# Triangular inversions on 64-wide diagonal blocks with a halved solve, and levels up to block 16 on four 32-wide tiles

## What is computed

```python
A = jnp.where(strict, jnp.einsum('bnhid,bnhjd->bnhij', kb, k) * gamma, 0.0)
T = lax.linalg.triangular_solve(A + eye, jnp.broadcast_to(eye, A.shape), left_side=True, lower=True, unit_diagonal=True)
u = T @ (v * beta[..., None])
w = T @ (kb * jnp.exp(g)[..., None])
...
def step(S, inp):
    u_n, w_n, qk_n, qd_n, kd_n, gt_n = inp
    v_new = u_n - jnp.einsum('bhck,bhkv->bhcv', w_n, S)
    o = jnp.einsum('bhck,bhkv->bhcv', qd_n, S) + jnp.einsum('bhij,bhjv->bhiv', qk_n, v_new)
    S = S * gt_n[..., None, None] + jnp.einsum('bhck,bhcv->bhkv', kd_n, v_new)
    return S, o
```

## Time and profile before

| | us |
|---|---|
| median of 3 runs | 2135.83 |
| lowest and highest | 2133.89, 2140.08 |
| the profiled execution, its own time | 2136.59 |
| its span in the trace | 2134.8 |
| TensorE busy in it | 1933.7 |
| VectorE busy in it | 606.0 |
| ScalarE busy in it | 316.7 |

### The profile page before, as it was taken

One profiled execution on the slowest core, in us unless ns is written; L12 is line 12 of the kernel. 1 busy time (PEld: TensorE's weight loads), 2 busy tenths in 40 slices (PEclk: granted clock), 3 DMA queues, 4 the chain that ended last, 5 costly groups with the idle time before them and its releaser, 6 DMA issues. The chain is left out here.

```text
span 2134.8 us, 36739 instructions
## 1 busy us (share of the span) xinstructions
PE 1933.7 (91%) x16513; PEld 1559.3 (73%) x16513; DVE 606.0 (28%) x1266; ACT 316.7 (15%) x639; POOL 41.1 (2%) x65
## 2 busy tenths in 40 slices
PE   5898987978999989878888879999999999999996
PEld 3786877877788868768787744456996699669953
DVE  4436565553200024635655310000000000100002
ACT  1012122220000014322222110000001100110011
POOL 0001000000000000000000000000000000000000
PEclk9999998989999999988999879999999999999999
DMA  9719431010443324100000079799999999999994
GB/s 352 281 63 427 171 158 80 1 80 9 158 158 147 129 112 174 40 6 11 11 11 6 1 322 387 276 390 428 425 421 420 428 425 417 428 426 425 408 429 191
DMA packets 37119, 492.75 MB, mean 231 GB/s; under 512 B 4379, under 2 KB 4540, under 8 KB 7324
## 3 DMA queue, kind: packets, MB, share of 16 engines
q1 hardware_dynamic: 36956, 490.33, 55.8%
HBM read 487.95 MB, written 2.36 MB: 230 GB/s over the span
## 5 line engine op out<-in xcount | busy, mean ns | idle before, releaser
L1946 PE MATMUL bank<-ring,arena 128*32 128x128 f32 x2016 | 227.6, 273 | 0.0
L1943 PE MATMUL bank<-ring,arena 128*32 128x384 f32 x2016 | 224.8, 487 | 2.5 <-DMA ring<-in_experts 2.5
L1946 PEld LDWEIGHTS bank<-ring,arena 128*32 128x32 f32 x2016 | 217.9, 110 | 0.0
L1938 PE MATMUL bank<-ring,arena 128*64 128x256 f32 x1792 | 204.8, 381 | 2.4 <-DMA ring<-in_experts 2.4
L1938 PEld LDWEIGHTS bank<-ring,arena 128*64 128x64 f32 x1792 | 126.2, 137 | 79.8 <-issue 22.7
L2140 DVE TENSOR_TENSOR arena<-bank,arena 128x256 f32<-128x256 f32 (+2 forms) x56 | 28.4, 508 | 545.3 <-PE bank L1946 154.8
L1229 PE MATMUL bank<-arena,ring 128*128 128x256 f32 x704 | 155.3, 382 | 4.0 <-DVE arena L290 3.8
L1229 PEld LDWEIGHTS bank<-arena,ring 128*128 128x128 f32 x704 | 134.0, 191 | 24.5 <-issue 4.1
L2096 ACT ACTIVATE arena<-bank 128x256 f32<-128x256 f32 (+2 forms) x56 | 25.3, 451 | 699.3 <-PE bank L1946 294.4
L1350 PE MATMUL bank<-arena,ring 128*128 128x256 f32 x512 | 115.6, 388 | 6.4 <-DVE arena L290 3.8
L1350 PEld LDWEIGHTS bank<-arena,ring 128*128 128x128 f32 x512 | 98.6, 194 | 24.8 <-issue 5.8
(11 more groups left out here) (368 smaller groups left out, 2506.3 us busy)
## 6 DMA issues: line engine op xcount, KB each, us to landing
ring<-in_experts SPq DMA_DIRECT2D x168, 2048.0 KB, 20.3
ring<-in_stream SPq DMA_DIRECT2D x61, 2048.0 KB, 11.0
arena<-in_masks SPq DMA_DIRECT2D x1, 1280.0 KB, 5.3
xT<-in_xT SPq DMA_DIRECT2D x1, 1024.0 KB, 6.1
arena<-in_s0gd SPq DMA_DIRECT2D x4, 256.0 KB, 3.3
out_sgd<-arena SPq DMA_DIRECT2D x4, 256.0 KB, 2.5
out_y<-arena SPq DMA_DIRECT2D x4, 256.0 KB, 2.5
arena<-in_hfw SPq DMA_DIRECT2D x1, 544.0 KB
```

The costliest lines, as they stand in the source:

```text
L1938: mm = nc.tensor.matmul(out[HALF * x:HALF * x + HALF, 0:256], h[:, j, 0:HALF], w[:, j, 256 * x:256 * x + 256], start=start, stop=stop, til ...
L1943: nc.tensor.matmul(out[lo:hi, 0:3 * P], h[:, j, lo:hi], w[:, j, 0:3 * P], start=start, stop=stop, tile_position=(0, lo), skip_group_check= ...
L1946: mm = nc.tensor.matmul(out[MID:P, r * P:(r + 1) * P], h[:, j, 32 * r:32 * r + 32], w[:, j, 3 * P:4 * P], start=(start and r == 0), stop=s ...
```

## The change

The inversion is now made on the two diagonal blocks of 64 of each 128 by 128 matrix. T, U and X hold two blocks on top of each other: 128 partitions, 64 columns for each q. LEVELS falls from 7 to 6, so levels 1 to 5 remain, and level 5 has the short form that level 6 had. Masks, copies and the strict scores shrink to 64 columns for each q (256 columns for four q instead of 512).

`pe_level` splits each product along the diagonal. For l up to 4 (blocks up to 16 joined into 32) it issues four matmuls of 32 by 32 with 32 columns on the tiles (0,0), (32,32), (64,64), (96,96) of the array; for l = 5 two of 64 by 64 with 64 columns on (0,0) and (64,64).

The rest of the triangular system is done by `pe_solve` in three steps: the diagonal blocks multiply the right-hand side; the off-diagonal block of A multiplies the solved half (one tile, (64a, 64b)); the other diagonal block multiplies that and adds to the first result in PSUM. After each step the half that is needed is copied, for g = 0 by ACT (`act_solve`), for g = 1 by DVE (`dve_solve`). The width of the right-hand side is 64 columns in the RWKV stage and 128 in the DeltaNet stage.

In the RWKV stage the right-hand sides are formed after level 3, in bank 7; TensorE waits there for the key norm of the next round (`s_krt`), and ACT copies both after both are done. The strict scores (now L998) are two matmuls of 64 by 64 columns on two column tiles instead of one of 128 by 128.

```diff
         class Inversion:
-            def __init__(self):
-                self.T = [take(4, T) for _ in range(2)]
-                self.U = [take(4, T) for _ in range(2)]
-                self.X = [take(4, T) for _ in range(2)]
+
+            def __init__(self, n):
+                self.n = n
+                self.T = [take(4, HB64) for _ in range(2)]
+                self.U = [take(4, HB64) for _ in range(2)]
+                self.X = [take(4, HB64) for _ in range(2)]
+                self.H = [take(4, n)] * 2
+                self.Z = [take(4, n) for _ in range(2)]
                 self.final = [self.U[0], self.T[1]]
...
             def dve_first(self, dve, r, g, low, up):
 
                 dve.wait_ge(s_id[g], 2 * (r + 1))
-                nc.vector.copy_predicated(self.T[g], self.level_mask(0, 0), low).then_inc(s_T[g], 1)
-                nc.vector.copy_predicated(self.U[g], self.level_mask(1, 0), up).then_inc(s_U[g], 1)
+                for dst, src, upper, done in ((self.T[g], low, 0, s_T[g]), (self.U[g], up, 1, s_U[g])):
+                    for rows, part in src:
+                        ins = nc.vector.copy_predicated(dst[rows], self.level_mask(upper, 0, rows), part)
+                    ins.then_inc(done, 1)
 
             def pe_level(self, pe, r, l, up):
+                w = 32 if 2 << l <= 32 else HB64
+                parts = [(slice(o, o + w), slice(o % HB64, o % HB64 + w), (o, o)) for o in range(0, P, w)]
+                column = lambda q, c: slice(q * HB64 + c.start, q * HB64 + c.stop)
                 for g in range(2):
                     pe.wait_ge(s_T[g], r * NT[g] + l)
                     for q in range(4):
-                        mm = nc.tensor.matmul(ps[g][:, q * T:(q + 1) * T], up[g][:, q], self.T[g][:, q], start=True, stop=True)
+                        for rows, c, at in parts:
+                            mm = nc.tensor.matmul(ps[g][rows, column(q, c)], up(g, q, rows, c), self.T[g][rows, q, c],
+                                                  start=True, stop=True, tile_position=at)
                     mm.then_inc(s_X[g], 1)
                 for g in range(2):
                     pe.wait_ge(s_U[g], r * NU[g] + l)
                     pe.wait_ge(s_Xs[g], r * (LEVELS - 1) + l)
                     if l < LEVELS - 1 or g == 1:
                         for q in range(4):
-                            mm = nc.tensor.matmul(ps[2 + g][:, q * T:(q + 1) * T], self.U[g][:, q], self.X[g][:, q],
-                                                  start=True, stop=True)
+                            for rows, c, at in parts:
+                                mm = nc.tensor.matmul(ps[2 + g][rows, column(q, c)], self.U[g][rows, q, c], self.X[g][rows, q, c],
+                                                      start=True, stop=True, tile_position=at)
                         mm.then_inc(s_TX[g], 1)
                     if l < LEVELS - 1 or g == 0:
                         for q in range(4):
-                            mm = nc.tensor.matmul(ps[4 + g][:, q * T:(q + 1) * T], self.X[g][:, q], self.U[g][:, q],
-                                                  start=True, stop=True)
+                            for rows, c, at in parts:
+                                mm = nc.tensor.matmul(ps[4 + g][rows, column(q, c)], self.X[g][rows, q, c], self.U[g][rows, q, c],
+                                                      start=True, stop=True, tile_position=at)
                         mm.then_inc(s_XU[g], 1)
 
...
-            def pe_final(self, pe, r, g):
-                pe.wait_ge(s_U[0] if g == 0 else s_T[1], (r + 1) * LEVELS)
-
-
+                                                  ps[4 + g][:, 0:4 * HB64].rearrange("p (q t) -> p q t", q=4)).then_inc(s_U[g], 1)
+
+            def pe_solve(self, pe, r, rhs, rhs_ready, lower):
+
+                n = self.n
+                for g in range(2):
+                    pe.wait_ge(s_U[0] if g == 0 else s_T[1], (r + 1) * LEVELS)
+                    rhs_ready(g)
+                    for q in range(4):
+                        for h in range(2):
+                            mm = nc.tensor.matmul(ps[g][blk(h), q * n:(q + 1) * n], self.final[g][blk(h), q], rhs[g][blk(h), q],
+                                                  start=(q == 0), stop=False, tile_position=(HB64 * h, HB64 * h), skip_group_check=True)
+                    mm.then_inc(s_Z[g], 1)
+                for g in range(2):
+                    a, b = g, 1 - g
+                    pe.wait_ge(s_Zs[g], 3 * r + 1)
+                    for q in range(4):
+                        mm = nc.tensor.matmul(ps[2 + g][blk(b), q * n:(q + 1) * n], lower[g][blk(a), q, blk(b)], self.Z[g][blk(a), q],
+                                              start=True, stop=True, tile_position=(HB64 * a, HB64 * b))
+                    mm.then_inc(s_Z[g], 1)
+                for g in range(2):
+                    b = 1 - g
+                    pe.wait_ge(s_Zs[g], 3 * r + 2)
+                    for q in range(4):
+                        mm = nc.tensor.matmul(ps[g][blk(b), q * n:(q + 1) * n], self.final[g][blk(b), q], self.H[g][blk(b), q],
+                                              start=False, stop=True, tile_position=(HB64 * b, HB64 * b), skip_group_check=True)
+                    mm.then_inc(s_Z[g], 1)
+
+            def solution_part(self, eng, r, g, k):
+
+                rows = blk(g if k == 0 else 1 - g)
+                dst = (self.H if k == 1 else self.Z)[g][rows].rearrange("p q v -> p (q v)")
+                eng.wait_ge(s_Z[g], 3 * r + k + 1)
+                return dst, ps[2 + g if k == 1 else g][rows, 0:4 * self.n]
+
+            def act_solve(self, act, r):
+                for k in range(3):
+                    dst, src = self.solution_part(act, r, 0, k)
+                    nc.scalar.activation(dst, src, ACT.Copy).then_inc(s_Zs[0], 1)
+
+            def dve_solve(self, dve, r):
+                for k in range(3):
+                    dst, src = self.solution_part(dve, r, 1, k)
+                    nc.vector.tensor_copy(dst, src).then_inc(s_Zs[1], 1)
+
+            def solved(self, eng, r):
+                for g in range(2):
+                    eng.wait_ge(s_Zs[g], 3 * r)
 
         drop(m_rw)
         m_keep = floats[0]
-        inv = Inversion()
+        inv = Inversion(RWN)
...
+                        if l == RHS_LEVEL:
+                            act.wait_ge(s_G, 2 * c + 2)
+                            for g in range(2):
+                                nc.scalar.activation(Gs[g].rearrange("p q v -> p (q v)"), ps[7][:, g * TT:(g + 1) * TT], ACT.Copy)\
+                                    .then_inc(s_Gs, 1)
+                    inv.act_solve(act, c)
...
-                            mm = nc.tensor.matmul(ps[4 + hh][:, s * T:(s + 1) * T], ar[g][:, 0, tok], bk[hh][:, 0, tok],
-                                                  start=True, stop=True)
+                            for h in range(2):
+                                part = slice(s * T + HB64 * h, s * T + HB64 * h + HB64)
+                                mm = nc.tensor.matmul(ps[4 + hh][blk(h), s * HB64:(s + 1) * HB64], ar[g][:, 0, part], bk[hh][:, 0, part],
+                                                      start=True, stop=True, tile_position=(0, HB64 * h))
...
-                    up = [AT[0][:, :, 0, :], Ab[1]]
+                    up = lambda g, q, rows, c: AT[0][rows, q, 0, rows] if g == 0 else Ab[1][rows, q, c]
...
+                        if l == RHS_LEVEL:
+                            for g in range(2):
+                                if g == 0:
+                                    pe.wait_ge(s_s0, 4 * c + 4)
+                                    if c < RWC - 1:
+                                        pe.wait_ge(s_krt, c + 2)
+                                for s in range(NS):
+                                    if s:
+                                        nc.tensor.matmul(ps[7][:, g * TT + T:(g + 1) * TT].rearrange("p (h v) -> p h v", h=2), ar[g][:, 0, T:TT],
+                                                         s0s[g], start=True, stop=False)
+                                    for hh in range(2):
+                                        q = 2 * s + hh
+                                        mm = nc.tensor.matmul(ps[7][:, g * TT + q * RWN:g * TT + (q + 1) * RWN], AT[g][:, q, 2, :],
+                                                              vtok[:, s, 64 * hh:64 * hh + 64], start=(s == 0), stop=(s == 0 or hh == 1))
+                                mm.then_inc(s_G, 1)
+                    inv.pe_solve(pe, c, Gs, lambda g: pe.wait_ge(s_Gs, 2 * c + g + 1), [AT[g][:, :, 0, :] for g in range(2)])
+                    inv.solved(pe, c + 1)
...
-                        low, up = (Ab[0], AT[0][:, :, 0, :]) if g == 0 else (AT[1][:, :, 0, :], Ab[1])
+                        diag = [(blk(h), AT[g][blk(h), :, 0, blk(h)]) for h in range(2)]
+                        whole = [(slice(0, P), Ab[g])]
```

(11 more changed lines are left out.)

111 lines of the change are left out of this document (47 added, 64 removed).

## The result

The changed kernel takes 2108.19 us in the median of 3 runs (2107.51 to 2116.76), 0.988 of before with an interval of 0.983 to 0.993. So it is faster, by some 28 us where 68 were forecast. The profiled execution is the slowest of the three, 2116.76 with a span of 2115.1.

What follows compares the result with a forecast made beforehand. TensorE's pace in the eight inversion windows was taken as the bound: 303.3 us there becomes 238.4, saving 64.9, and scores save 3.5; 2136.6 less 68.4 gives 2068.2 us, range 2012 to 2140.

Steps and rivals of the forecast that it cites:

- The bound and the levels: Levels 1 to 4: instruction supply sets TensorE's pace, 1.54 packets at 3.23 us each, 4.96 us a level.
- The credit of 1.6 us: Levels 1 to 4 of a round: half a packet is already there when TensorE arrives, taken off 19.8 us.
- The fast rival: Levels 1 to 4: instruction supply keeps up, a level takes 2.95 us, 119 us saved, 2017 us in all; chance 0.20.
- Packet stops: Levels 1 to 4: each packet stops TensorE, a level takes 7.4 us, 2146 us in all, slower; chance 0.18.
- low clock on every pair: Levels 1 to 4: every record pair takes 59.7 ns, a level 11.5 us, 2276 us in all; chance 0.04.
- The tails: Level 5 and solve: 5.7 us (RWKV) and 8.4 us (DeltaNet) a round, plus 2.2 and 2.8 for lower clock.
- The right-hand sides and the norms: RWKV levels 1 to 4: right-hand sides add 0.5 us, VectorE's norms part of their time, 20.0 us a round in all.
- The DeltaNet levels: DeltaNet levels 1 to 4: 20.5 us a round, with 2.3 charged for the norm that holds VectorE 4.8 us.
- The scores: Strict scores in the RWKV rounds: two column tiles at L345's pace cost half, saving 3.5 us in all.
- The clock: In the inversions: lower level, 1.2 of 2.4 GHz, costing little in the levels, 2.2 (RWKV) or 2.8 us (DeltaNet) in tails.
- clock low throughout: Rest of the tails doubles too (+20 us), as much again in products behind them, 2108 us in all; chance 0.12.
- The prediction's 4.8 us a level: Levels 1 to 4 by the skill page: 192 matmuls of 25 ns, sum some 6 us lower than the forecast.

Runs made afterwards that it cites:

- second profile: The changed kernel run once more, unchanged, as yardstick: 2107.4 us in the median, 2110.5 us in the profiled execution.
- e4_w64_split: Changed kernel with 64-wide tiles at levels 1 to 4, each matmul cut into two of 32 columns: 2278.0 us, ratio 1.066 to the kernel before.
- e12_w64_warm: Changed kernel with 64-wide tiles, grouped scores, DeltaNet norm in pieces, plus unused matmuls filling TensorE's waits: 2029.2 us, ratio 0.949 to the kernel before.

## Why the prediction was right and wrong

The forecast gain of 68 us came out at 28. The limit was named rightly; what failed are terms beside it that were put at next to nothing or half: the right-hand sides and norms between the levels, the strict scores, and the outputs at a lower clock.

*The bound and the levels: right.* TensorE's pace in the windows was the thing to price, and late instructions were its limit. In round i = 0, which has no norm, the four levels take 21.07 us, 5.27 each, where a packet of 3.23 us and 1.54 packets a level had given 4.96. The credit of 1.6 us for half a packet that is there when TensorE arrives did not show: 18.2 us was the forecast for such a round. The packets rose by 38, as forecast (with 2,464 more matmuls; the 2,432 of the prediction leave out those of the strict scores). The fast rival is what the levels do between stops: a level without one takes 3.1 us (c = 0, level 4). "Packet stops" and "low clock on every pair" didn't come.

*The tails: right*, 32.0 against 31.6 and 41.5 against 44.8.

*The right-hand sides and the norms: wrong*, the largest miss: the RWKV levels took 19.9 us more. The step was "the right-hand sides add 40 records (0.5 us)", as if long matmuls ran in time that TensorE would otherwise wait. They take 4.45 us a round at the lower clock, and the run that moves them out finds 2.4 of that in the way, where 0.5 was priced: 7.6 us in four rounds. The other 12 were not taken apart by a run, but the trace shows what stands there. The products of the norms (L949, L954 and L958, each in three rounds of four) take 9.1 us, where they took 3.9 at the upper clock before; only VectorE's part was counted. And in three rounds TensorE waits 1.8 us at level 1 for ACT's copy of X, which did not stand out before. In c = 0, TensorE and then ACT:

```profile
235.31 0.65 PE L729 MATMUL bank<-arena 32*32 32x32 f32 x32 [1.80 <-ACT arena L742]
```

```profile
234.47 0.42 ACT L877 ACTIVATE arena<-arena 128x256 f32<-128x256 f32 x1 [4.13 <-DVE arena L1072]
234.80 0.64 ACT L742 ACTIVATE arena<-bank 128x256 f32<-128x256 f32 x2
```

The copy (L742) stands on ACT behind the square of the next key (L877), which waits for VectorE. Against all this, TensorE stops less, 17.2 us in the four rounds, 4.3 each, where i = 0 has 8.5. In none of the 25 stops was a packet long in store: it began at most 1.7 us before TensorE ran out, the one at 317.2 half a microsecond. A long matmul hides the arrival of one packet, and the next short batches wait again: in c = 1 the packet of 321.7 came under the right-hand sides without a stop, and the next, of 327.6, ended a stop at 330.06.

*The DeltaNet levels*: 7.4 us over, and not by the norm. It was charged with 2.3 us, half of the time for which it holds VectorE. In three rounds TensorE waited 1.4 to 3.4 us for the copies behind it (L749) and spent some 1.9 on its product (L1602), but its stops fell from 8.5 to about 4.5 us. Its waits in i = 0 and in i = 2:

```profile
PE bank L729 <- issue: 4.7, 4, 1.8
PE bank L720 <- issue: 3.8, 2, 2.9
```

```profile
PE bank L729 <- issue: 3.4, 2, 2.3
PE bank L720 <- DVE arena L749: 3.3, 1, 3.3
...
PE bank L720 <- issue: 1.3, 1, 1.3
```

So the levels of these rounds (21.4, 23.6 and 23.3 us) are 1.7 us longer than those of i = 0 in the mean, less than the 2.3. What was short is the base of 18.2 us, by 2.9 in i = 0; 1.1 of that is a wait at level 1 for VectorE's level 0 (L709).

*The scores: wrong in sign*, -3.5 forecast, +10.6 measured (+7.7 in the second profile). The step was to take L345's pace for two column tiles. L345 runs 128 records of one form; the strict scores stand between full-array matmuls, and 32 times 0.24 us, 7.7, go to the change of form. What is left goes with a lower clock in the first two rounds (0.85 and 0.82, before 1.00 and 0.89); it was not taken apart.

*The clock: right in the windows* (0.62 to 0.69), unpriced behind them (the outputs, 4.9 us). The rival "clock low throughout" named 2108 and the result is 2108. That is a coincidence of two sums: with the clock up ahead of each inversion, the windows stay at 263 us, and 13 us come back outside them, not 40.

Together, by the cuts of the table: 67.6 us forecast, less 24.4 in the windows, 14.1 at the scores, 4.9 at the outputs and 4.0 elsewhere (within the scatter of executions), leaves 20.2; the spans differ by 19.7.

The Trainium skill, page TensorEngine Tiling (Array Packing), section Performance Considerations, advises against a tiling factor from a dimension that is already small, and it is borne out here: the windows are 42 us shorter with 64-wide tiles. Its reason is not: by about 60 cycles a matmul, 16 matmuls would take 0.4 us at the upper level and 0.8 at the lower (an estimate from that page), and the batches took 0.42 at the lower. The prediction's 4.8 us a level from that page counts the two records of a matmul as two matmuls; by the 96 matmuls of a level it is 2.4 (an estimate from that page). Against the 4.96 of the prediction, its 4.8 us make 5 us over 32 levels, not 6. What spoiled the small tiles was the number of instructions, and with it went the lower clock.

## What to carry to other kernels

Count instructions, not only columns, before cutting a matmul into more tiles: where TensorE consumes a packet of some 250 in less time (1.7 us here, 127 matmul records at 13.3 ns) than the next takes to arrive (2.2 to 2.8 us), the program runs at the pace of the packets, and the sign is an "issue" stop in the middle of a batch without a semaphore. Long work put between such batches is hidden only in part: of 4.45 us a round 2.4 stood in the way here. Keep tiles of one form in one run, and compare a price taken from another line with the neighbours of that line.

## What the runs showed of the hardware

- A record on a 64-wide tile takes the same 53 ns at the lower clock level with 32 columns (e4_w64_split) as with 64 (0.86 us for 16 in e12_w64_warm); halving the columns there buys nothing. On 32-wide tiles 32 columns take 13.3 ns at the same level.
- Column tiles of 64 columns take 65 ns a record alternating with full-array matmuls and 39 ns in a run of 16.
- The clock follows what TensorE did just before: unused matmuls in a wait of 5 us took the following scores from a granted clock of 0.71 to 1.00, and all such fillings together were worth 22 us of 2052. Short bursts between waits let it fall again (1.00, 1.00, 0.71, 0.50 behind one filled wait).
